# State-space keys: four tiles' sums in one bank, their rows spread by a product, segment sums turned

## The chip, the core and the metric

The kernel is one program on one core of a Trainium2 chip. The metric is the device time of one execution in microseconds (us), the median of several runs. The core has TensorE (PE: matrix products; its weight loads are listed apart as PEld), VectorE (DVE), ScalarE (ACT), GpSimd (POOL), and a queue on SyncE that starts the weight transfers.

## What is computed

Two blocks follow each other, on 256 positions of width 1024: first a block with forgetting attention, selected attention and two layers of retrieved experts, then a block of two layers, each made of a gated feed-forward, a mixer, and another feed-forward. The change touches only the mixer of the second block, which runs twice (stages `ssd0` and `ssd1`):

```python
proj = h @ w_in                                   # z, xbc, dt, q, k, v
dt  = softplus(dt_raw + dt_bias);  adt = dt * -exp(a_log)
a_cum = cumsum(adt)                               # inside chunks of 128 positions, 16 heads
seg   = a_cum[l] - a_cum[s]
lmat  = where(l >= s, exp(seg), 0)
y_diag = einsum(C_l . B_s, lmat, x_s * dt_s)      # 4 groups of 4 heads, 2 chunks
...                                               # state between chunks, gate, norm
q = rms_norm(q per head of 64) ; k = rms_norm(k per head of 64)
y_att = dilated_attention(q, k, v)
x = x + concat(y_ssd, y_att) @ w_out
```

`seg` for a pair l, s is the sum of `adt` over the positions between them, and that is how the kernel makes it: as a product with 0/1 triangles.

## The kernel before

Every weight tile is 128x1024 in float32 (512 KB), streamed by the SyncE queue through a ring of five. ACT copies each tile to a rounded half `HI` (L525), DVE subtracts to get `LOW` (L538), and TensorE multiplies both with the activations `HT`, which are split in the same way: 24 products of 256 columns for a projected tile (`project`, L882), all in the fp32r format. ACT makes HI two tiles ahead and DVE makes LOW one tile ahead of the one being multiplied (`feed`).

There is no scheduler: each engine's order is that of its own program below, and semaphores (`c.by(event)`) tie them. A product's result goes to one of four PSUM banks, P4 to P7, taken first in, first out by `open_bank`; who opens a bank waits until its last reader has freed it. A bank opened with `held=True` is out of the turn until `leave_bank`. P0 to P3 hold long sums.

In a mixer stage the order on TensorE is: norm and turning of the input, 16 tiles `sx`, one `sd` (the steps dt), 8 slots `sz`, and then the loop that the change is in: for i in 0..7 one key tile is projected, one group of four heads gets its segment sums (`segments`, L2736, one bank), and the group before gets its `diagonal` product (L2716). The 8 query tiles follow, then 8 value slots and the attention. Round the loop:

- `steps(i)` on POOL (L3095) makes the moving data of the segment sums: gt times adt for four heads, 128x512. It waits for `segments(i-2)`, since there are two buffers.
- ACT copies the key tile and squares it (L2856, L2857), then takes exp of the segment sums (L2880).
- DVE multiplies that by C.B (`decayed`, L3023), for which `diagonal(i)` waits.
- after every second tile `key_sums(p)` (L2723) sums the squares of two tiles over each head and spreads them over the head's rows in the same product (128x512); DVE makes means of them (L2992), ACT the root (L2862), DVE the reciprocal (L2998) and the scaling of the two key tiles (L3000).
- at the loop's start DVE copies dt and adt out of PSUM (L2977) and makes `xd` = x dt for both chunks (L2985); ACT's first key copy waits for the second of these, and its exp `ea` of the cumulated steps (L2874) comes after that; POOL's `xe` (L3110) waits for `ea`.

Of the kernel before, what the change touches and what calls it, by code (L numbers as in the profile page):

```python
# [28 lines left out]
def shape_constants():  # L29
# [1328 lines left out]
def arena_parts(s, places):  # L1358
# [7 lines left out]
    if s[:3] == "ssd":  # L1366
        return [[("a", 26624 + places[s]["width"], F32), ("h", 4096, F32R), ("l", 4096, F32R)]]
# [1290 lines left out]
def ssd_tensor(pe, c, s):  # L2658
# [65 lines left out]

    for i in range(8):
# [86 lines left out]
def ssd_scalar(act, c, s):  # L2812
# [51 lines left out]
    for i in range(8):
# [64 lines left out]
def ssd_vector(dve, c, s):  # L2929
# [58 lines left out]
    def key_means(p):  # L2988
        dve.wait_ge(*c.by(s, "key_sums", p))
        if p >= 2:  # L2990
            dve.wait_ge(*c.by(s, "keys_normed", p - 2))
        dve.tensor_scalar(f.rr2[p % 2], c.psum(s, "key_sums", p), 1.0 / 64, EPS, ALU.mult, ALU.add).then_inc(  # L2992
            *c.dve.at((s, "key_means", p), ("free", s, "key_sums", p)))

    def key_norm(p):
        rr = f.rr2[p % 2]
        dve.wait_ge(*c.by(s, "key_root", p))
        dve.reciprocal(rr, rr).then_inc(*c.dve.at((s, "key_inverse", p)))  # L2998
        dve.wait_ge(*c.by(s, "key_inverse", p))
        dve.scalar_tensor_tensor(out=f.pair(p), in0=f.pair(p), scalar=f.gain, in1=rr, op0=ALU.mult,  # L3000
                                 op1=ALU.mult).then_inc(*c.dve.at((s, "keys_normed", p)))
# [12 lines left out]
    for i in range(8):  # L3014
# [218 lines left out]
```

## Time and profile before

| | us |
|---|---|
| median of 3 runs | 3196.69 (3194.41 to 3196.91) |
| profiled execution, its own time | 3195.49 |
| its span, first to last instruction | 3193.7 |
| PE busy in the span | 3140.6 (98%) |
| DVE busy | 2531.2 (79%) |
| ACT busy | 1682.2 (53%) |
| POOL busy | 466.6 (15%) |

The span is a profile of one execution. An engine's busy time counts its instructions' durations, waits for a shared resource inside an instruction included. The loop that the change is in takes 2216.7 to 2264.9 us in the first mixer stage and comes again 621.4 us later in the second, with the same durations to a few hundredths of a microsecond.

### The profile page before, as it was taken

How to read it: one execution, taken by the hardware profiler on the slowest of the kernel's cores; microseconds unless marked ns; L12 is line 12 of the kernel's file. 1: busy time of each engine (PE TensorE's matmuls, PEld its weight loads, DVE VectorE, ACT ScalarE, POOL GpSimd, SP SyncE). 2: the span in 40 equal slices, each digit the busy share in tenths (PEclk: the TensorE clock that was granted, in tenths of full speed). 3: DMA queues.
4: the chain of work that ended last, by engine and by line, in shares of the span. 5: the costliest groups of instructions: out<-in, count | busy, mean ns of one | idle time of the engine just before them, and what ended most of it. 6: DMA issues, size and time to landing. Idle time of an engine off the chain costs nothing.

```text
span 3193.7 us, 52741 instructions
## 1 busy us (share of the span) xinstructions
PE 3140.6 (98%) x20327; PEld 2733.2 (86%) x20327; DVE 2531.2 (79%) x4361; ACT 1682.2 (53%) x2698; POOL 466.6 (15%) x317
## 2 busy tenths in 40 slices
PE   7999999999999999999999999999999999999999
PEld 7799988888888679988888888889978888898787
DVE  7879999888878679999877777758777677687775
ACT  4455555544455564555555555456654454566543
POOL 0268100000000458300000000002140000022200
PEclk9999999999999999999999999999999999999999
DMA  9445455577766225445566555554435555544355
GB/s 346 171 139 182 146 166 178 200 268 254 259 203 247 73 95 185 159 152 178 172 218 213 191 191 177 188 178 164 139 121 190 191 181 187 177 145 151 130 188 171
DMA packets 160312, 579.91 MB, mean 182 GB/s; under 512 B 18368, under 2 KB 20160, under 8 KB 160064
## 3 DMA queue, kind: packets, MB, share of 16 engines
q1 hardware_dynamic: 155952, 567.60, 52.6%
q10 hardware_dynamic: 3600, 8.37, 0.7%
q8 instruction: 164, 2.69, 0.3%
q0 software_dynamic: 512, 0.57, 0.1%
q14 instruction: 84, 0.69, 0.1%
HBM read 574.89 MB, written 1.05 MB: 180 GB/s over the span
## 4 chain that ended last, share of the span: by engine, by line
PE 92%; DVE 5%; issue 1%; ACT 1%; DMA 1%; POOL 0%; ACTq 0%; SPq 0%; DVEq 0%
PE P L2189 22%; PE P L893 17%; PE P L956 12%; PE P L2166 12%; PE P L896 9%; PE P L882 8%; PE P L2153 2%; DVE LOW L538 1%; PE P L861 1%; PE P L920 1%; PE P L1138 1%; PE P L1152 1%; PE P L981 1%; PE P L864 1%; PE P L795 1%
## 5 line engine op out<-in xcount | busy, mean ns | idle before, releaser
L538 DVE TENSOR_TENSOR LOW<-RING,HI 128x1024 fp32r<-128x1024 f32 x880 | 1078.0, 1228 | 152.5 <-ACT HI L525 151.3
L525 ACT ACTIVATE HI<-RING 128x1024 fp32r<-128x1024 f32 x984 | 1032.6, 1052 | 288.2 <-DMA RING<-in_pv 83.8
L893 PE MATMUL P<-HT,HI 128*128 128x512 f32 x2368 | 590.9, 391 | 0.0
L893 PEld LDWEIGHTS P<-HT,HI 128*128 128x128 f32 x2368 | 433.4, 188 | 83.6 <-issue 1.0
L896 PEld LDWEIGHTS P<-HT,LOW 128*128 128x128 f32 x2368 | 323.0, 190 | 23.1
L896 PE MATMUL P<-HT,LOW 128*128 128x256 f32 x2368 | 330.2, 282 | 0.0
L2166 PE MATMUL P<-HT,HI 128*128 128x256 f32 x2048 | 282.4, 286 | 0.0
L538 POOL TENSOR_TENSOR LOW<-RING,HI 128x1024 fp32r<-128x1024 f32 x104 | 252.1, 2431 | 89.0 <-ACT HI L525 88.7
L2166 PEld LDWEIGHTS P<-HT,HI 128*128 128x128 f32 x2048 | 258.7, 192 | 0.1
L882 PE MATMUL P<-HT,HI 128*128 128x256 f32 x1728 | 233.5, 288 | 0.0
L882 PEld LDWEIGHTS P<-HT,HI 128*128 128x128 f32 x1728 | 216.3, 192 | 9.0 <-issue 4.2
L904 DVE TENSOR_REDUCE peer_a<-P 128x256 f32<-128x512 f32 x128 | 88.2, 689 | 108.5 <-PE P L896 108.2
L752 POOL TENSOR_SCALAR STAT<-STAT 128x1 f32<-128x1 f32 x10 | 6.1, 613 | 1068.1 <-DVE STAT L759 564.2
L2472 DVE TENSOR_TENSOR peer_a<-peer_a 128x256 f32<-128x256 f32 x256 | 159.1, 622 | 1.0 <-ACT peer_a L2260 1.0
L2263 ACT ACTIVATE peer_a<-P 128x256 f32<-128x256 f32 x128 | 49.2, 384 | 182.5 <-PE P L2166 182.5
L2166 PE MATMUL P<-HT,LOW 128*128 128x256 f32 x1024 | 143.7, 283 | 0.0
L2189 PE MATMUL P<-LOW,peer_wh 128*128 128x512 f32 x512 | 143.1, 401 | 0.0
L2253 ACT ACTIVATE peer_a<-P 128x512 f32<-128x512 f32 x128 | 76.4, 597 | 125.8 <-PE P L2153 125.8
L631 POOL MEMSET ACC<- 128x1024 f32 x10 | 10.1, 1005 | 893.9 <-PE P L2153 548.6
L2189 PE MATMUL P<-HI,peer_wh 128*128 128x512 f32 x512 | 137.1, 389 | 1.6 <-ACT peer_wh L2272 1.6
L2189 PE MATMUL P<-HI,peer_wl 128*128 128x512 f32 x512 | 136.8, 389 | 0.0
L2189 PE MATMUL P<-HI,peer_wh_latex 128*128 128x512 f32 x496 | 135.5, 394 | 0.0
(437 smaller groups left out, 5315.1 us busy)
## 6 DMA issues: line engine op xcount, KB each, us to landing
RING<-in_pu SPq DMA_DIRECT2D x256, 512.0 KB, 3.3
RING<-in_pv SPq DMA_DIRECT2D x256, 512.0 KB, 3.3
RING<-in_fgA SPq DMA_DIRECT2D x44, 512.0 KB, 3.3
RING<-in_fuA SPq DMA_DIRECT2D x44, 512.0 KB, 3.2
RING<-in_fdA SPq DMA_DIRECT2D x44, 512.0 KB, 3.2
RING<-in_fgB SPq DMA_DIRECT2D x44, 512.0 KB, 3.3
RING<-in_fuB SPq DMA_DIRECT2D x44, 512.0 KB, 3.3
RING<-in_fdB SPq DMA_DIRECT2D x44, 512.0 KB, 3.2
```

Of the source, the lines that this page charges most:

```text
L525: act.activation(c.his[i % NHL], c.raw[m % NR], ACT.Copy).then_inc(*c.hi.at(("hi", m)))
L538: eng.tensor_tensor(c.low[m % NR], c.raw[m % NR], c.his[i % NHL].bitcast(F32), ALU.subtract).then_inc(*sig.at(("lo", m)))
L882: m = pe.matmul(ps[:, 0:256], w[:, k * 128:k * 128 + 128], c.ht[h][:, k, :], start=i == 0 and k == 0, stop=i == 2 and k == 7)
L893: pe.matmul(ps, hi[:, k * 128:k * 128 + 128], c.both[:, :, k, :], start=k == 0, stop=False)
L896: m = pe.matmul(ps[:, 0:256], lo[:, k * 128:k * 128 + 128], c.ht[0][:, k, :], start=False, stop=k == 7)
L904: dve.tensor_reduce(dst, ps, AX.X, ALU.add).then_inc(*c.dve.at(event, ("free", name, j)))
L956: m = pe.matmul(c.y[q], lhs[1 if i == 1 else 0][:, t * 128:t * 128 + 128], (lo if i == 2 else hi)[:, hf * 512:hf * 512 + 512], start=i == ...
L2153: m = pe.matmul(ps[:, 64 * t:64 * t + 64], f.is_row[g % 2][:, t // SIDE, :, t % SIDE], f.share[g % 2][q][:, t // SIDE, :, t % SIDE], start ...
L2166: m = pe.matmul(ps[:, 0:256], w[:, k * 128:k * 128 + 128], c.ht[h][:, k, :], start=i == 0 and k == 0, stop=i == 2 and k == 7)
L2189: m = pe.matmul(c.y[q], (f.wl(j) if i == 1 else f.wh(j))[:, t * 128:t * 128 + 128], (lo if i == 2 else hi)[:, hf * 512:hf * 512 + 512], st ...
L2253: act.activation(dst, c.psum(s, "gates", part, g).rearrange("p (t j) -> p t j", t=8), ACT.Copy, scale=1.0 / SHARE).then_inc(*c.act.at((s, ...
L2472: dve.tensor_tensor(ge, ge, f.gate_of(j), ALU.mult).then_inc(*c.dve.at((s, "weighed", j)))
```

## The change

Four edits, in the mixer stages alone.

1. **Segment sums turned.** The stationary and the moving side change places: gt, as `later`, is the stationary operand once for all heads, and le times adt moves, 128x512 for four heads. The data are now fp32r, and so that nothing is lost adt is split in two parts, `ad2`, both of which go through the product: two products of 512 columns instead of four float32 ones of 128. `steps` on POOL writes 128x1024 instead of 128x512, and DVE makes `ad2` with two small instructions before `xd`. POOL makes `later` (128x128) at the stage's start.
2. **Sums of four tiles in one bank.** `key_sums(i)` runs for each tile with 256 columns; four of them add into one held bank, each tile's heads in rows of its own. The existing helpers `heads_root_scalar` (ACT, L1029 before) and `heads_inverse_vector` (DVE, L1035 before) then take one root and one reciprocal of 256 columns for four tiles.
3. **Rows spread.** `key_rows(p)` spreads the reciprocals back over 128 rows for two tiles: two products of 256 columns in fp32r, on `both_rows`, which holds a rounded part and its remainder in rows of the same tile, made by two DVE instructions after the reciprocal. POOL makes the stationary `rows_of` (128x512) at the stage's start. `key_norm` reads the factors from PSUM.
4. **Room.** The packed constants of a mixer stage (loaded on ACT's queue in the feed-forward before) grow by 737 columns of float32.

```diff
@@ Ssd
-        self.wb = [c.at(s, 24576 + 512 * n, 512) for n in range(2)]
+        steps = c.arena[s, "h"]
+        self.wb = [steps[:, 1024 * n:1024 * n + 1024] for n in range(2)]
+        self.later = c.arena[s, "l"][:, 0:128]
+        self.ad2 = c.arena[s, "l"][:, 128:192]
@@ ssd_tensor
-    def key_sums(p):
-        ps = open_bank(pe, c, s, "key_sums", p)
-        pe.wait_ge(*c.by("squares", f.sqk, 8 + 2 * p + 1))
-        pe.matmul(ps, bd64, f.sq2[p % 2], start=True, stop=True).then_inc(*c.pe.at((s, "key_sums", p)))
+    def key_sums(i):
+        j = 8 + i
+        b, q = divmod(j, 4)
+        if q == 0:
+            open_bank(pe, c, "heads_sums", f.sqk, b, held=True)
+        pe.wait_ge(*c.by("squares", f.sqk, j))
+        pe.matmul(c.psum("heads_sums", f.sqk, b)[:, 0:256], f.pack("headsum")[:, 96 - 32 * q:224 - 32 * q], f.sq[j % 4],
+                  start=q == 0, stop=q == 3).then_inc(*c.pe.at(("head_sums", f.sqk, j)))
+        if q == 3:
+            leave_bank(c, "heads_sums", f.sqk, b)
+
+    def key_rows(p):
+        b, half = divmod(p, 2)
+        ps = open_bank(pe, c, s, "key_rows", p)
+        pe.wait_ge(*c.by(s, "both_rows", b))
+        pe.wait_ge(*c.by(s, "rows_of"))
+        for q in (2 * half, 2 * half + 1):
+            m = pe.matmul(ps[:, q % 2 * 256:q % 2 * 256 + 256], f.rows_of[:, 128 * q:128 * q + 128], f.both_rows[b],
+                          start=True, stop=True)
+        m.then_inc(*c.pe.at((s, "key_rows", p)))
...
-        for r in range(4):
-            m = pe.matmul(ps[:, r * 128:r * 128 + 128], f.wb[i % 2][:, r * 128:r * 128 + 128], f.le, start=True, stop=True)
+        for half in range(2):
+            m = pe.matmul(ps, f.later, f.wb[i % 2][:, 512 * half:512 * half + 512], start=half == 0, stop=half == 1)
...
-        if i >= 2 and i % 2 == 0:
-            key_sums(i // 2 - 1)
+        if i:
+            key_sums(i - 1)
+        if i == 7:
+            key_rows(0)
     project(pe, c, f.sqk, 0)
     diagonal(7)
...
-    key_sums(3)
+    key_sums(7)
+    key_rows(1)
...
+        if j in (3, 4):
+            key_rows(j - 1)
@@ ssd_scalar
-        if i >= 2 and i % 2 == 0:
-            key_root(i // 2 - 1)
+        if i == 5:
+            heads_root_scalar(act, c, f.sqk, 2, f.rr[0], c.const("eps"))
...
         if j == 0:
-            key_root(3)
+            heads_root_scalar(act, c, f.sqk, 3, f.rr[1], c.const("eps"))
@@ ssd_vector
+    dve.wait_ge(*c.by(s, "dt"))
+    dve.tensor_copy(f.ad2[:, 0:32], f.dts[:, 32:64]).then_inc(*c.dve.at())
+    dve.wait_ge(*c.dve.last())
+    dve.tensor_tensor(f.ad2[:, 32:64], f.dts[:, 32:64], f.ad2[:, 0:32].bitcast(F32), ALU.subtract).then_inc(
+        *c.dve.at((s, "steps_halves")))
...
+    def key_inverse(b):
+        rr = f.rr[b]
+        heads_inverse_vector(dve, c, f.sqk, 2 + b, rr)
+        dve.wait_ge(*c.by("heads_inverse", f.sqk, 2 + b))
+        dve.tensor_copy(f.rr_hi, rr).then_inc(*c.dve.at())
+        dve.wait_ge(*c.dve.last())
+        dve.scalar_tensor_tensor(out=f.both_rows[b], in0=f.rr_hi.bitcast(F32), scalar=f.pack("lowrow"), in1=rr,
+                                 op0=ALU.mult, op1=ALU.add).then_inc(*c.dve.at((s, "both_rows", b)))
...
-        if i >= 3 and i % 2:
-            key_norm(i // 2 - 1)
...
-        if i >= 2 and i % 2 == 0:
-            key_means(i // 2 - 1)
+        if i == 6:
+            key_inverse(0)
...
         if j == 0:
-            key_means(3)
+            key_norm(0)
+            key_norm(1)
             carried(0)
             carried(1)
+        if j == 1:
+            key_inverse(1)
...
-        if j == 4:
-            key_norm(3)
+        if j in (4, 5):
+            key_norm(j - 2)
@@ ssd_pool
-        pool.tensor_tensor(f.wb[i % 2].rearrange("p (r s) -> p r s", r=4), f.gt.unsqueeze(1).broadcast_to([128, 4, 128]),
-                           f.ad[:, ch, 4 * g:4 * g + 4].unsqueeze(2).broadcast_to([128, 4, 128]), ALU.mult).then_inc(
+        ad = f.ad2.bitcast(F32).rearrange("p (q t h) -> p q t h", q=2, t=2)[:, :, ch, 4 * g:4 * g + 4]
+        pool.tensor_tensor(f.wb[i % 2].rearrange("p (q r l) -> p q r l", q=2, r=4),
+                           f.le.unsqueeze(1).unsqueeze(1).broadcast_to([128, 2, 4, 128]),
+                           ad.unsqueeze(3).broadcast_to([128, 2, 4, 128]), ALU.mult).then_inc(
             *c.pool.at((s, "steps", i)))
 
     pool.wait_ge(*c.by(s, "legt"))
+    pool.tensor_tensor(f.later, f.gt, f.gt, ALU.mult).then_inc(*c.pool.at((s, "later")))
+    pool.wait_ge(*c.by(s, "pack"))
+    pool.tensor_scalar(f.rows_of, f.pack("hsel2"), 1.0, None, ALU.mult).then_inc(*c.pool.at((s, "rows_of")))
...
-    pool.wait_ge(*c.by(s, "dt"))
+    pool.wait_ge(*c.by(s, "steps_halves"))
     steps(0)
     steps(1)
```

Three places in the order of the instructions. First POOL, from the norm of a mixer stage (L752 before, L756 after) to the loop, as it stands before:

```order
L752 TENSOR_SCALAR STAT<-STAT 128x1 [waits s_pool_done,s_act_done,s_dve_done,s_pe_done]
L3102 TENSOR_TENSOR ssd_a<-ssd_a 128x1024 [waits s_pool_done,s_tables_landed,s_act_done,s_dve_done,s_pe_done]
L3102 TENSOR_TENSOR ssd_a<-ssd_a 128x1024 [waits s_act_done]
L3095 TENSOR_TENSOR ssd_a<-ssd_a 128x512 [waits s_dve_done]
L3095 TENSOR_TENSOR ssd_a<-ssd_a 128x512
L3110 TENSOR_TENSOR ssd_a<-ssd_a 128x1024 [waits s_act_done,s_dve_done]
```

and with the change (L3135 is `later`, L3137 `rows_of`, L3129 `steps`, L3148 `xe`):

```order
L756 TENSOR_SCALAR STAT<-STAT 128x1 [waits s_pool_done,s_act_done,s_dve_done,s_pe_done]
L3135 TENSOR_TENSOR ssd_l<-ssd_a 128x128 [waits s_pool_done,s_act_done,s_tables_landed,s_dve_done,s_pe_done]
L3137 TENSOR_SCALAR ssd_l<-ssd_a 128x512 [waits s_pack_landed]
L3140 TENSOR_TENSOR ssd_a<-ssd_a 128x1024 [waits s_act_done] x2
L3129 TENSOR_TENSOR ssd_h<-ssd_a,ssd_l 128x1024 [waits s_dve_done]
L3129 TENSOR_TENSOR ssd_h<-ssd_a,ssd_l 128x1024
L3148 TENSOR_TENSOR ssd_a<-ssd_a 128x1024 [waits s_act_done,s_dve_done]
```

Two instructions now stand right behind the norm's, and each `steps` is twice as wide.

Second DVE at the start of the loop, before (L2977 takes dt out of PSUM, L2985 makes `xd`, L538 makes LOW of the second key tile, L3023 is `decayed(0)`):

```order
L2977 COPY ssd_a<-P 128x64 [waits s_pe_done]
L2985 TENSOR_TENSOR ssd_a<-ssd_a 128x1024 [waits s_act_done,s_dve_done]
L2985 TENSOR_TENSOR ssd_a<-ssd_a 128x1024 [waits s_act_done]
L538 TENSOR_TENSOR LOW<-RING,HI 128x1024 [waits s_hi_made]
L3023 TENSOR_TENSOR ssd_a<-ssd_a 128x512 [waits s_dve_done,s_act_done]
```

and with the change:

```order
L3004 COPY ssd_a<-P 128x64 [waits s_pe_done]
L3006 CAST ssd_l<-ssd_a 128x32 [waits s_dve_done]
L3008 TENSOR_TENSOR ssd_l<-ssd_a,ssd_l 128x32 [waits s_dve_done]
L3017 TENSOR_TENSOR ssd_a<-ssd_a 128x1024 [waits s_act_done,s_dve_done]
L3017 TENSOR_TENSOR ssd_a<-ssd_a 128x1024 [waits s_act_done]
L542 TENSOR_TENSOR LOW<-RING,HI 128x1024 [waits s_hi_made]
L3053 TENSOR_TENSOR ssd_a<-ssd_a 128x512 [waits s_dve_done,s_act_done]
```

Two small instructions came in ahead of `xd`.

Third TensorE from the segment sums of i = 5 to the key tile of i = 6, before (L2736 segment sums, L2716 diagonal product, L882 a projected tile; P4 to P7 are the banks):

```order
L2736 MATMUL P7<-ssd0_a 128x128 [waits s_pool_done,s_act_done]
L2736 MATMUL P7<-ssd0_a 128x128 x3
L2716 MATMUL P2<-ssd0_a 128x64 [waits s_act_done,s_dve_done]
L2716 MATMUL P2<-ssd0_a 128x64 x3
L882 MATMUL P6<-HT,HI 128x256 [waits s_hi_made,s_act_done]
```

and with the change, from the last sum of the first four tiles on (L2735 is `key_sums`, L2761 the segment sums, L2725 the diagonal product, L886 a projected tile):

```order
L2735 MATMUL P6<-ssd0_a 128x256 [waits s_act_done]
L886 MATMUL P7<-HT,HI 128x256 [waits s_hi_made,s_act_done]
L886 MATMUL P7<-HT,HI 128x256 x15
L886 MATMUL P7<-HT,LOW 128x256 [waits s_lo_made]
L886 MATMUL P7<-HT,LOW 128x256 x7
L2761 MATMUL P4<-ssd0_h,ssd0_l 128x512 [waits s_pool_done,s_act_done]
L2761 MATMUL P4<-ssd0_h,ssd0_l 128x512
L2725 MATMUL P2<-ssd0_a 128x64 [waits s_act_done,s_dve_done]
L2725 MATMUL P2<-ssd0_a 128x64 x3
L2735 MATMUL P5<-ssd0_a 128x256 [waits s_act_done]
L886 MATMUL P6<-HT,HI 128x256 [waits s_hi_made,s_act_done]
```

The key tile of i = 6 now goes into P6, the bank in which the sums of the first four tiles stood, and whose reader is ACT's root at i = 5.

## Rows read from the trace of the kernel before

**Rows 1.** The page: busy us, share of the span, instructions.

```profile
PE 3140.6 (98%) x20327; PEld 2733.2 (86%) x20327; DVE 2531.2 (79%) x4361; ACT 1682.2 (53%) x2698; POOL 466.6 (15%) x317
```

**Rows 2.** The chain of waits from 2215 to 2275 us: start us, us, what.

```profile
2214.83 1.59 PE P L956 x7
...
2229.20 0.89 PE P L2736 x8
...
2230.94 1.78 PE P L2747 x8
...
2233.58 2.87 PE P L882 x24
...
2242.84 0.91 PE P L2723 x2
...
2247.51 0.84 PE P L2716 x8
...
2264.93 2.87 PE P L882 x24
```

**Rows 3.** Timeline at the loop's start, DVE, POOL, ACT: start us, us, engine, line.

```profile
2216.80 0.23 DVE L2977 COPY ssd_a<-P 128x64 f32<-128x64 f32 x1 [2.39 <-PE P L2703]
2217.06 3.21 DVE L2985 TENSOR_TENSOR ssd_a<-ssd_a 128x1024 f32<-128x1024 f32 x2
2217.11 4.06 POOL L3095 TENSOR_TENSOR ssd_a<-ssd_a 128x512 f32<-128x512 f32 x2 [10.00 <-DVE ssd_a L2977]
...
2220.19 2.06 DVE L538 TENSOR_TENSOR LOW<-RING,HI 128x1024 fp32r<-128x1024 f32 x1
2220.35 0.38 ACT L2856 ACTIVATE ssd_a<-P 128x256 f32<-128x256 f32 x1 [2.09 <-DVE ssd_a L2985]
...
2222.32 0.20 ACT L2874 ACTIVATE ssd_a<-P 128x32 f32<-128x32 f32 x1
...
2222.66 1.91 POOL L3110 TENSOR_TENSOR ssd_a<-ssd_a 128x1024 f32<-128x1024 f32 x1 [1.49 <-ACT ssd_a L2874]
...
2223.04 2.07 DVE L3023 TENSOR_TENSOR ssd_a<-ssd_a 128x512 f32<-128x512 f32 x1 [0.79 <-ACT ssd_a L2880]
```

**Rows 4.** The instructions of L3095 and L2985: ns min/median/max.

```profile
L3095 POOL TENSOR_TENSOR ssd_a<-ssd_a x16: 1041/1265/2082, 2217.1 to 2869.0; 128x512 f32<-128x512 f32 x16
...
L2985 DVE TENSOR_TENSOR ssd_a<-ssd_a x4: 1224/1643/2064, 2217.1 to 2839.6; 128x1024 f32<-128x1024 f32 x4
```

**Rows 5.** Timeline of ACT in the loop at i = 5.

```profile
2251.66 0.38 ACT L2857 ACTIVATE ssd_a<-P 128x256 f32<-128x256 f32 x1
2252.21 0.60 ACT L2880 ACTIVATE ssd_a<-P 128x512 f32<-128x512 f32 x1 [0.17 <-PE P L2736]
2252.82 1.28 ACT L2862 ACT_TABLE_LOAD   x1
```

**Rows 6.** ACT's root of 256 columns in the first block.

```profile
L1029 ACT ACTIVATE mix_a<-P,mix_a x5: 455/475/478, 104.0 to 1055.3; 128x256 f32<-128x256 f32 x5
```

**Rows 7.** Timeline at the mixer stage's norm.

```profile
2136.50 0.76 POOL L752 TENSOR_SCALAR STAT<-STAT 128x1 f32<-128x1 f32 x1 [189.00 <-DVE STAT L759]
...
2137.89 0.56 DVE L767 TENSOR_SCALAR ssd_a<-X,STAT 128x640 f32<-128x640 f32 x1
...
2138.57 1.04 PE L795 MATMUL P<-CST,ssd_a 128*128 128x128 f32 x8
```

**Rows 8.** Timeline at the first stage's norm.

```profile
10.37 1.47 POOL L631 MEMSET ACC<- 128x1024 f32 x1
...
11.08 1.10 DVE L767 TENSOR_SCALAR mix_a<-X,STAT 128x640 f32<-128x640 f32 x1
```

**Rows 9.** POOL's instructions of L1345, L1346, L538: ns min/median/max.

```profile
L1345 POOL TENSOR_SCALAR mix_a<-mix_a,STAT x40: 604/606/1500, 133.4 to 1141.3; 128x128 f32<-128x128 f32 x40
...
L1346 POOL TENSOR_SCALAR mix_a<-mix_a,STAT x40: 922/927/1677, 134.1 to 1141.9; 128x256 f32<-128x256 f32 x40
...
L538 POOL TENSOR_TENSOR LOW<-RING,HI x104: 2377/2406/2916, 164.3 to 1312.2; 128x1024 fp32r<-128x1024 f32 x104
```

More of the change, by code:

```diff
@@ L38, in shape_constants @@
     c["bd64"] = (p[:, None] // 64 == p[None, :] // 64).astype(f)
+    c["headsum"] = np.zeros((128, 224), f)
+    c["headsum"][:, 96:128] = c["bd64"][:, 48:80]
+    c["hsel2"] = 2 * c["hsel"]
+    c["lowrow"] = -(p[:, None] % 16 // 8).astype(f)
     c["le"] = (p[:, None] <= p[None, :]).astype(f)
@@ L1366, in arena_parts @@
     if s[:3] == "ssd":
-        return [[("a", 26624 + places[s]["width"], F32), ("h", 4096, F32R), ("l", 4096, F32R)]]
+        return [[("a", 25600 + places[s]["width"], F32), ("h", 4096, F32R), ("l", 4096, F32R)]]
     return [[("a", 32768, F32), ("ij", 512, F16), ("g2", 512, F16), ("iota", 128 * SIDE, F16), ("iota16", 128, F16),
@@ L2627, in __init__ @@
         self.sq = [c.at(s, 4096 + 256 * n, 256) for n in range(4)]
-        self.sq2 = [c.at(s, 4096 + 512 * n, 512) for n in range(2)]
         self.junk = c.at(s, 5120, 1024)
-        self.rr2 = [c.at(s, 22024 + 512 * n, 512) for n in range(2)]
+        self.rr = [c.at(s, 22024 + 256 * n, 256) for n in range(2)]
         self.d = [c.at(s, 23048 + 256 * n, 256) for n in range(5)]
@@ L2637, in __init__ @@
         self.ad = self.dts[:, 32:64].rearrange("p (t h) -> p t h", t=2)
-        self.wb = [c.at(s, 24576 + 512 * n, 512) for n in range(2)]
-        self.eb = [c.at(s, 25600 + 512 * n, 512) for n in range(2)]
-        self.pack = lambda n: c.packed(s, s, 26624, n if n == "bd64" else f"{n}_{l}")
+        steps = c.arena[s, "h"]
+        self.wb = [steps[:, 1024 * n:1024 * n + 1024] for n in range(2)]
+        self.later = c.arena[s, "l"][:, 0:128]
+        self.ad2 = c.arena[s, "l"][:, 128:192]
+        self.eb = [c.at(s, 24576 + 512 * n, 512) for n in range(2)]
+        self.pack = lambda n: c.packed(s, s, 25600, n if n in ("bd64", "headsum", "hsel2", "lowrow") else f"{n}_{l}")
+        self.both_rows = [c.arena[s, "l"][:, 192 + 256 * n:448 + 256 * n] for n in range(2)]
+        self.rr_hi = c.arena[s, "l"][:, 704:960]
+        self.rows_of = c.arena[s, "l"][:, 1024:1536]
         self.an, self.gain = c.stat(4, 1), c.stat(5, 1)
@@ L2806, in ssd_loads @@
 def ssd_loads(act, c, s):
-    act.dma_start(c.at(s, 26624, c.places[s]["width"]), c.ins[f"pack_{s}"]).then_inc(*c.landed["pack"].at((s, "pack")))
+    act.dma_start(c.at(s, 25600, c.places[s]["width"]), c.ins[f"pack_{s}"]).then_inc(*c.landed["pack"].at((s, "pack")))
     act.dma_start(c.at(s, 18944, 256), c.ins["legt"]).then_inc(*c.landed["tables"].at((s, "legt")))
@@ L2869, in ssd_scalar @@
         if i >= 4:
-            act.wait_ge(*c.by(s, "key_sums", i // 2 - 2))
+            act.wait_ge(*c.by("head_sums", f.sqk, 4 + i))
         copied(8 + i, f.kt[:, i, :])
@@ L2986, in ssd_vector @@
                           ALU.mult).then_inc(*c.dve.at((s, "xd", t)))
[L2988 to L2993, printed above, removed]
-    def key_norm(p):
[L2996 to L3001, printed above, removed]
+    def key_inverse(b):
[6 more added lines that the diff above has]
+                                 op0=ALU.mult, op1=ALU.add).then_inc(*c.dve.at((s, "both_rows", b)))
+    def key_norm(p):
+        dve.wait_ge(*c.by("copied", f.sqk, 8 + 2 * p + 1))
+        dve.wait_ge(*c.by(s, "key_rows", p))
+        dve.scalar_tensor_tensor(out=f.pair(p), in0=f.pair(p), scalar=f.gain, in1=c.psum(s, "key_rows", p), op0=ALU.mult,
+                                 op1=ALU.mult).then_inc(*c.dve.at((s, "keys_normed", p), ("free", s, "key_rows", p)))
     def gate(t, hf):
```

7 lines of the change are left out of this document (2 added, 5 removed).

## The prediction

> **What bounds the kernel now.** I read the page first: TensorE is busy for 98% of the span and POOL for 15% [rows 1], so time is TensorE's products plus its few waits. Then the chain of waits over the loop of the first mixer stage: it runs from one TensorE group to the next with almost nothing between. A projected tile costs 2.87 us for 24 products (0.12 each of 256 columns), a group's segment sums 0.89, the diagonal product 0.84, a key sum of 512 float32 columns 0.91, four float32 products of 256 columns 1.78 (0.445 each), and seven fp32r products of 512 columns 1.59 (0.23 each) [rows 2]. Last the timeline, for what stands around TensorE [rows 3, 5, 7]. The work of DVE and ACT that goes (reciprocals and roots of 512 columns) is hidden behind TensorE and is worth nothing by itself. Both mixer stages behave alike, so I cost one and take it twice.
>
> **TensorE's own work.** Segment sums: four float32 products of 128 columns at 0.89 become two fp32r products of 512 columns, 2 x 0.23 = 0.46. That is 0.43 less, eight times: **-3.4 us**. Key sums: four of 0.91 are 3.6, eight of 0.445 are 3.6: **0**. Key rows are new: eight fp32r products of 256 columns at 0.12: **+1.0**. If nothing waited, a stage would gain 2.4 us, and two stages 4.9.
>
> **A mechanism that the rest hangs on.** DVE and POOL do not run side by side here. POOL's two `steps` of 128x512 took 4.06 us together at the loop's start, while DVE's two `xd` took 3.21 [rows 3]; the same instructions take 1.04 and 1.22 each elsewhere [rows 4]. The four ran by turns: xd(0) to 2218.3, steps(0) to 2219.2, xd(1) to 2220.3, steps(1) to 2221.2. L538 behind them took 2.06, where `xd` of the same width takes 1.22, and `decayed(0)` took 2.07, since it was held until POOL's `xe` ended at 2224.57 [rows 3]. Whoever waits longer goes first, and then needs its own time less about 0.14 that was spent at the door.
>
> **Wait 1, the loop's start.** `steps` is now 128x1024, which the trace does not show. The nearest is `xe`, also 128x1024 with a repeated operand: 1.91 [rows 3]. So 0.87 more for each, which DVE sees in full. Ahead of `xd` DVE gets two small instructions, about 0.4 us with hand-off, by the 0.23 of the copy before them [rows 3]. I follow the turns:
> - xd(0) ends at 2218.6, steps(0) at 2220.4 (TensorE was ready for it at 2220.0), xd(1) at 2221.5, steps(1) at 2223.2, and LOW of the second key tile at 2224.3 instead of 2222.25.
> - TensorE: segment sums 2220.45 to 2220.9, the HI part of the next tile until 2222.85, then it stands for LOW until 2224.35, 1.5 us; tile done at 2225.35, next sums at 2225.8.
> - `ea` comes 1.2 later, since ACT's first copy waits for xd(1); `xe` gets its turn after LOW and ends at 2226.1, `decayed(0)` at 2226.65. In the trace it ended at 2225.11 [rows 3]: the diagonal product starts **1.5 us later**, even though two groups of segment sums (2 x 0.43) are already saved.
> - On to the fourth key tile: third sums save 0.43, two small key sums stand for one large, and `decayed(1)`, behind two more wide `steps`, costs about 0.35. That tile started at 2233.58 [rows 2]; I get 2234.95, 1.35 later. With the three savings of 0.43 that makes waits of **+2.7 us**.
> From there POOL has 4.6 us a turn for 1.9 of work, and `steps` is ahead again.
>
> **Wait 2, a bank.** The sums of the first four tiles stay in P6 until ACT's root at i = 5 has read them, and the key tile of i = 6 opens just P6. In the trace ACT squares the tile (0.38), takes exp (0.60), and loads the table for the root at once behind it, 1.28 us [rows 5]. Ahead of the square lies a copy of the same tile, about 0.3. Counted from the end of the key tile of i = 5: square done at 0.7, exp at 1.3, table 2.55, root 3.0 (0.475 for 256 columns [rows 6]). TensorE is through its sums (0.46), diagonal (0.84 [rows 2]) and key sum (0.445) at 1.75. It stands **+1.3 us**. Before, the root read no bank, and this wait did not exist.
>
> **Wait 3, the norm.** At the stage's start POOL now runs `later` and `rows_of` right behind its norm instruction, which ends at 2137.26; DVE's L767 is issued at 2137.89 and TensorE's second turning waits for it [rows 7]. `later` ends near 2137.7, so `rows_of` is under way when L767 comes. That this pair collides the first stage shows: with a POOL instruction from 10.37 to 11.84, L767 took 1.10 instead of 0.56 [rows 7, 8]. `rows_of` is a TENSOR_SCALAR of 512 columns: 128 columns take 0.604 and 256 take 0.922 [rows 9], so 512 take 1.56. Floor: POOL's 1.47 [rows 8] is a memset of 1024 columns, so 512 could take half, 0.73. L767 then ends 1.25 or 0.4 later. If DVE slips in between the two, it is nothing. I take the nearest kind, **+1.25 us**.
>
> **Hidden.** DVE's new instructions at i = 6 (reciprocal of half the columns, cast, combination, some 2.3 us) end about 0.6 us before `key_rows(0)` needs them. At j = 0 `carried` reopens the bank of `key_rows(0)` just as `key_norm(0)` frees it, with 0.2 us to spare. The larger constants load, 377 KB more, lies in the feed-forward before and goes beside a ring of five tiles. If any of these covers were gone, it would cost tenths.
>
> **The sum.** One stage: -3.4 + 0 + 1.0 + 2.7 + 1.3 + 1.25 = +2.8; with the unrounded values 2.7. Two stages: +5.4. The profiled execution took 3195.49, which makes 3200.9; the median of the runs is 1.2 above it, so there 3202.1.
>
> **Rivals.**
> - *Forecast, all three waits*, 3202 with a range of 3199 to 3206: 0.50. About 6 of 10 of it lies below the mark of +0.2%.
> - *The norm wait is small or absent*, because `rows_of` runs at half the memset's time or DVE goes first. Then 2 x 0.85 to 2 x 1.25 less, about 3200, and down to 3197 if the small casts are cheap as well: 0.25. For it: only 0.2 us decide who goes first.
> - *Waits hidden, the arithmetic counts*: two stages at -2.4 and some tenths that TensorE now stands at `decayed(0)`, 3191. It needs LOW of the second key tile and the root in time, and both rows speak against that: 0.05.
> - *Slower*: a wide `steps` takes more than 1.9. POOL's L538, with two full operands, takes 2.38 [rows 9]. Four `steps` lie on the path at the loop's start, so 0.1 more for each is 0.4 in a stage and 0.8 in all. From 2.04 us for each the kernel is over the mark, and at 2.4 it takes 3206: 0.20. Against it: `steps` repeats both operands, and at 512 columns took 1.04, which with `xe` at 1.91 lies on one line.
>
> The Trainium skill's page "GPSIMD Engine Reference", section "Elementwise — side-by-side cycle accounting", would have the slower case: it measures a float32 `tensor_tensor` of 2048 columns on this engine at 4.5 us, as an estimate 2.25 for 1024. By that the sum would be +2.8 us more, 3205. The trace's `xe` took 1.91 for that width [rows 3], so I keep the row.
>
> **How the numbers follow.** What a measurement of this kernel can tell from no change is about 0.2%, 6.4 us: 3190.3 and 3203.1. Of the forecast 0.31 lies within and 0.19 over; the small norm wait adds 0.25 within; the slower rival 0.20 less a little over; the hidden case 0.04 faster, and the rest within. Faster 0.04, same 0.60, slower 0.36. The range leaves out the hidden case below and the worst of the slow one: 3194 to 3208.
>
> **What the profile will show.** Segment sums at 0.46 and eight key sums at 0.445; POOL's 128x1024 `steps` at 1.9 alone and 3 and more beside DVE; PE idle before the LOW part of the second key tile, about 1.5, released by DVE; PE idle of 1.3 before the key tile of i = 6, released by ACT's root; L767 at 1.0 to 1.8 in mixer stages. Wrong it would be if the first wait is not there, since it is half of the waits; if ACT loads the root's table elsewhere; or if TensorE's granted clock falls in the gaps.

## The result: 4.6 us longer, a ratio of 1.0016

The changed kernel took 3200.75 us (median of 18 runs, 3197.81 to 3204.94), the kernel before 3196.12 (18 runs beside it, 3191.55 to 3197.89). The ratio is 1.0016, with a 95% interval of 1.0009 to 1.0022: slower by 4.6 us, and inside the 0.2% that the forecast called the same. The forecast was 3202.1. The profiled execution took 3199.65, with a span of 3197.8.

The page of after; the first row answers to [rows 1]. Busy time of DVE and ACT fell by 9 and 16 us, that of POOL rose by 18. None of the three says what happened to the time.

```profile
PE 3137.5 (98%) x20263; PEld 2729.2 (85%) x20263; DVE 2522.1 (79%) x4361; ACT 1666.6 (52%) x2686; POOL 484.3 (15%) x321
```

The chain of waits of after over the same loop as in [rows 2] (start us, us, what). The fourth key tile starts at 2234.23; counted from the first key tile it started 16.88 in before and starts 18.41 in after (the first tiles start at 2216.70 and 2215.82 in the two timelines). A group of segment sums is 0.47 instead of 0.89, a key sum 0.49 twice for 0.91 once, and key rows are 0.23. From the fourth key tile on one stretch leaves TensorE: from 2246.45 to 2249.44 the chain lies on ACT. (Over the first three tiles it lies mostly on DVE.)

```profile
2233.79 0.43 PE P L2735 x2
2234.23 2.87 PE P L886 x24
2237.09 0.47 PE P L2761 x2
2237.56 0.84 PE P L2725 x8
2238.40 0.49 PE P L2735 x2
...
2247.04 0.61 ACT ssd_a L2907
2247.66 1.28 ACT L1033
2248.96 0.48 ACT ssd_a L1033
2249.44 0.04 issue
2249.48 3.13 PE P L886 x24
...
2259.06 0.23 PE P L2746 x2
```

The waits of TensorE in the same loop of after (us in total, times, longest). In before this view had one row, 0.2 us of L2716 for L3023.

```profile
PE P L886 <- ACT ssd_a L1033: 1.3, 1, 1.3
PE P L886 <- DVE LOW L542: 1.2, 1, 1.2
PE P L2725 <- DVE ssd_a L3053: 0.8, 2, 0.6
PE P L2761 <- POOL ssd_h L3129: 0.3, 1, 0.3
```

The timeline of after at the loop's start, TensorE, DVE and POOL; it answers to [rows 3]. TensorE's HI part of the second key tile ends at 2222.24 and its LOW part starts at 2223.45, since L542 runs from 2220.49 to 2223.41: it shares the time with the second wide `steps` (L3129) and then with `xe` (L3148). The first `decayed` (L3053) takes 2.37 beside `xe`.

```profile
2216.51 4.05 DVE L3017 TENSOR_TENSOR ssd_a<-ssd_a 128x1024 f32<-128x1024 f32 x2
2220.49 2.92 DVE L542 TENSOR_TENSOR LOW<-RING,HI 128x1024 fp32r<-128x1024 f32 x1
2223.34 2.37 DVE L3053 TENSOR_TENSOR ssd_a<-ssd_a 128x512 f32<-128x512 f32 x1
...
2216.67 5.65 POOL L3129 TENSOR_TENSOR ssd_h<-ssd_a,ssd_l 128x1024 fp32r<-128x1024 f32 x2 [10.42 <-DVE ssd_l L3008]
2222.96 2.21 POOL L3148 TENSOR_TENSOR ssd_a<-ssd_a 128x1024 f32<-128x1024 f32 x1 [0.64 <-ACT ssd_a L2901]
...
2220.16 2.08 PE L886 MATMUL P<-HT,HI 128*128 128x256 f32 x16
2223.45 1.21 PE L886 MATMUL P<-HT,LOW 128*128 128x256 f32 x8 [1.22 <-DVE LOW L542]
2224.51 0.63 PE L2761 MATMUL P<-ssd_h,ssd_l 128*128 128x512 f32 x2
2225.76 1.11 PE L2725 MATMUL P<-ssd_a 128*128 128x64 f32 x8 [0.63 <-DVE ssd_a L3053]
```

At the norm the timeline of after (DVE, then POOL) answers to [rows 7]: L771 is issued at 2136.80, 0.17 after `rows_of` (L3137) began, and takes 0.79, not 0.56. It ends at 2137.59, half a microsecond before `rows_of` does.

```profile
2136.80 0.79 DVE L771 TENSOR_SCALAR ssd_a<-X,STAT 128x640 f32<-128x640 f32 x1
...
2135.42 0.76 POOL L756 TENSOR_SCALAR STAT<-STAT 128x1 f32<-128x1 f32 x1 [189.00 <-DVE STAT L763]
2136.26 0.40 POOL L3135 TENSOR_TENSOR ssd_l<-ssd_a 128x128 fp32r<-128x128 f32 x1
2136.63 1.51 POOL L3137 TENSOR_SCALAR ssd_l<-ssd_a 128x512 fp32r<-128x512 f32 x1
```

**A table by stage.** The runs of one kernel spread over 7 us, so single effects of a microsecond are read from the traces. I took the first start of five kinds of TensorE work in the first mixer stage of each profiled execution, and of the norm after it; the second stage agrees within 0.1 us. Columns are us: the norm's turning to the first cumulative sum, to the first state product, to the first `carried`, to the turning of y, to the next stage's norm, and the sum. The medians stand last.

| kernel | to sums | to states | to carried | to y | to norm | stage | median |
|---|---|---|---|---|---|---|---|
| before | 82.4 | 11.1 | 32.2 | 31.0 | 88.0 | 244.7 | 3196.12 |
| after | 82.5 | 13.0 | 31.8 | 31.4 | 88.5 | 247.2 | 3200.75 |
| root ahead of exp | 82.5 | 13.1 | 30.1 | 31.5 | 88.4 | 245.6 | 3197.02 |
| steps at half width | 82.5 | 11.4 | 31.8 | 31.4 | 88.5 | 245.6 | 3197.54 |
| copies behind skip | 82.3 | 13.1 | 31.7 | 31.4 | 88.5 | 247.0 | 3201.11 |
| segment sums alone | 82.3 | 13.0 | 30.7 | 30.9 | 88.0 | 244.9 | 3196.84 |
| keys alone | 82.3 | 11.5 | 33.8 | 31.4 | 88.4 | 247.4 | 3201.14 |
| 31 columns | 82.6 | 13.0 | 31.8 | 31.4 | 88.0 | 246.8 | 3199.04 |
| three edits | 82.4 | 13.0 | 30.2 | 31.4 | 88.0 | 245.0 | 3195.78 |
| and `xd` late | 82.4 | 10.2 | 30.1 | 31.3 | 88.0 | 242.0 | 3191.07 |

The stage of after is 2.5 us longer than that of before, 5.0 for two; the medians say 4.6. TensorE's granted clock was 1.00 in the loop of both (2216 to 2264), so it did not fall in the gaps.

### The profile page after: what moved, and what is told of

It reads as the page before. It is cut to its first block, busy times and chain, and to the rows that moved or that the text cites. A ratio compares the mean times of both kernels' runs of the same rounds, so it can differ in the third digit from the quotient of the medians.

```text
span 3197.8 us, 52611 instructions
## 1 busy us (share of the span) xinstructions
PE 3137.5 (98%) x20263; PEld 2729.2 (85%) x20263; DVE 2522.1 (79%) x4361; ACT 1666.6 (52%) x2686; POOL 484.3 (15%) x321
## 3 DMA queue, kind: packets, MB, share of 16 engines
HBM read 575.64 MB, written 1.05 MB: 180 GB/s over the span
## 4 chain that ended last, share of the span: by engine, by line
PE 91%; DVE 5%; issue 1%; ACT 1%; DMA 1%; POOL 0%; SPq 0%; DVEq 0%; ACTq 0%
PE P L2193 22%; PE P L897 17%; PE P L960 12%; PE P L2170 11%; PE P L900 9%; PE P L886 8%; PE P L2157 2%; DVE LOW L542 1%; PE P L865 1%; PE P L924 1%; PE P L1142 1%; PE P L1156 1%; PE P L985 1%; PE P L868 1%; PE P L799 1%
## 5 line engine op out<-in xcount | busy, mean ns | idle before, releaser
L542 DVE TENSOR_TENSOR LOW<-RING,HI 128x1024 fp32r<-128x1024 f32 x880 | 1081.2, 1231 | 150.9 <-ACT HI L529 150.4
L542 POOL TENSOR_TENSOR LOW<-RING,HI 128x1024 fp32r<-128x1024 f32 x104 | 252.0, 2429 | 89.1 <-ACT HI L529 88.9
L886 PE MATMUL P<-HT,HI 128*128 128x256 f32 x1728 | 231.7, 287 | 2.6 <-ACT ssd_a L1033 2.6
L886 PEld LDWEIGHTS P<-HT,HI 128*128 128x128 f32 x1728 | 216.5, 192 | 9.8 <-ACT ssd_a L1033 3.4
L756 POOL TENSOR_SCALAR STAT<-STAT 128x1 f32<-128x1 f32 x10 | 6.1, 612 | 1068.4 <-DVE STAT L763 564.3
L2264 ACT ACTIVATE peer_a<-peer_a 128x256 f32<-128x256 f32 x128 | 53.2, 416 | 165.8 <-DVE peer_a L908 165.8
```

The lines of the kernel that those rows point to most:

```text
L542: eng.tensor_tensor(c.low[m % NR], c.raw[m % NR], c.his[i % NHL].bitcast(F32), ALU.subtract).then_inc(*sig.at(("lo", m)))
L886: m = pe.matmul(ps[:, 0:256], w[:, k * 128:k * 128 + 128], c.ht[h][:, k, :], start=i == 0 and k == 0, stop=i == 2 and k == 7)
```

## The experiments

Each was run beside the kernel before; the first four together (before: 3195.94 there, 33 runs), the last four together (3195.75, 33 runs), each kernel 11 times. A diff shows the edit's core.

**Root ahead of exp.** Is TensorE's wait at i = 6 the bank that the root holds?

```diff
@@ ssd_scalar, for i in range(8)
         feed(act, c, "act", f.sqk, 8 + i)
+        if i == 5:
+            heads_root_scalar(act, c, f.sqk, 2, f.rr[0], c.const("eps"))
...
-        if i == 5:
-            heads_root_scalar(act, c, f.sqk, 2, f.rr[0], c.const("eps"))
```

> ACT takes the root of the first four tiles at the start of i = 5, ahead of that tile's copy, instead of behind its exp. Theory (the bank P6 is held by a late root): the wait of 1.3 us before the key tile of i = 6 is gone in both stages, with nothing in its place, since the table loads now fall into the time of the projection: 2.6 us less than the changed kernel, about 3198.2. Rival (the lost time lies in the arithmetic of key sums and key rows, or in transfers, and TensorE would only wait elsewhere): no change, 3200.8.

3197.02, ratio 1.0008 (0.9998 to 1.0017); the stretch to `carried` is 1.7 us shorter. The chain of this run goes through the place on TensorE alone:

```profile
2245.45 0.84 PE P L2725 x8
2246.28 0.49 PE P L2735 x2
2246.77 2.86 PE P L886 x24
2249.64 0.47 PE P L2761 x2
```

The bank was the wait. It gave back 1.6 per stage, more than the 1.3 that the view of waits lists, and than the 1.3 that I had expected.

**Steps at half width.** What do the wide `steps` cost at the loop's start? POOL makes only the first half of each, and both products read that half, so the second part of the step sizes is not in the sums.

```diff
-        pool.tensor_tensor(f.wb[i % 2].rearrange("p (q r l) -> p q r l", q=2, r=4),
-                           f.le.unsqueeze(1).unsqueeze(1).broadcast_to([128, 2, 4, 128]),
-                           ad.unsqueeze(3).broadcast_to([128, 2, 4, 128]), ALU.mult)
+        pool.tensor_tensor(f.wb[i % 2][:, 0:512].rearrange("p (r l) -> p r l", r=4),
+                           f.le.unsqueeze(1).broadcast_to([128, 4, 128]),
+                           ad[:, 0, :].unsqueeze(2).broadcast_to([128, 4, 128]), ALU.mult)
...
-            m = pe.matmul(ps, f.later, f.wb[i % 2][:, 512 * half:512 * half + 512], start=half == 0, stop=half == 1)
+            m = pe.matmul(ps, f.later, f.wb[i % 2][:, 0:512], start=half == 0, stop=half == 1)
```

> POOL writes only the first half of the steps (128x512); both products read that half, so TensorE's work is the same and the segment sums are twice the rounded part. Theory (DVE and POOL take turns, and the wide steps push xd, LOW and decayed back): steps take 1.04 alone, the wait for LOW of the second key tile falls from 1.2 to under 0.5, the fourth key tile starts 1.6 us sooner in each stage: 3.2 us less, about 3197.6. Rival (the two small DVE instructions and the order of the queues make the wait, whatever POOL's width): under 0.5 us less, 3200.5.

3197.54, ratio 1.0004 (0.9995 to 1.0013); the stretch to the states is 1.6 shorter. The wait for LOW is gone; that for the first `decayed` is longer than in after:

```profile
PE P L886 <- ACT ssd_a L1033: 1.3, 1, 1.3
PE P L2725 <- DVE ssd_a L3053: 1.2, 1, 1.2
```

So the width is 1.6 of what the loop's start costs. The rest stays with `steps` of the old width. In this run's timeline the first `decayed` is issued 0.80 after DVE fell idle, waiting for ACT's exp, and takes 2.07 beside `xe`, as in before (0.79 and 2.07 in [rows 3]); counted from the first key tile it comes 6.67 in, where it came 6.34 in before. TensorE gets there two groups of segment sums sooner, 0.84, and waits.

**Copies behind skip.** The two small products of POOL at the stage's start go behind its products with the skip weights.

```diff
@@ ssd_pool
     pool.wait_ge(*c.by(s, "legt"))
-    pool.tensor_tensor(f.later, f.gt, f.gt, ALU.mult).then_inc(*c.pool.at((s, "later")))
-    pool.wait_ge(*c.by(s, "pack"))
-    pool.tensor_scalar(f.rows_of, f.pack("hsel2"), 1.0, None, ALU.mult).then_inc(*c.pool.at((s, "rows_of")))
     for t in range(2):
...
+    pool.tensor_tensor(f.later, f.gt, f.gt, ALU.mult).then_inc(*c.pool.at((s, "later")))
+    pool.wait_ge(*c.by(s, "pack"))
+    pool.tensor_scalar(f.rows_of, f.pack("hsel2"), 1.0, None, ALU.mult).then_inc(*c.pool.at((s, "rows_of")))
     pool.wait_ge(*c.by(s, "steps_halves"))
```

> POOL makes later and rows_of after the two skip products, when it is idle before the loop, instead of behind the norm. By the trace of the changed kernel L771 took 0.79 in mixer stages and 0.55 elsewhere, so 0.2 us less in each stage, 0.4 in all, about 3200.3, and L771 back at 0.55. By the price in my prediction, where the loser stands for the whole of rows_of, it would be 2.5 us less, 3198.3.

3201.11, ratio 1.0013 (1.0004 to 1.0022); the stage is 0.2 shorter. L771 of this run, beside that of after (ns min/median/max), is back at its time without company:

```profile
L771 DVE TENSOR_SCALAR ssd_a<-X,STAT x2: 553/554/556, 2139.1 to 2762.9; 128x640 f32<-128x640 f32 x2
```

```profile
L771 DVE TENSOR_SCALAR ssd_a<-X,STAT x2: 783/786/790, 2136.8 to 2760.8; 128x640 f32<-128x640 f32 x2
```

The collision costs 0.2 and not 1.25: at that price this kernel would have stood near 3198.3. And it is not `rows_of` as such that holds L771 back. The run with the keys alone (below) has no `later`; there `rows_of` (L3129 in that kernel) starts 0.54 ahead of L771 and runs a microsecond past its issue, and L771 takes 0.55, its time alone:

```profile
2137.08 1.56 POOL L3129 TENSOR_SCALAR ssd_l<-ssd_a 128x512 fp32r<-128x512 f32 x1
2137.62 0.55 DVE L771 TENSOR_SCALAR ssd_a<-X,STAT 128x640 f32<-128x640 f32 x1
```

In the run with the segment sums alone `later` stands by itself, ends 0.15 before the same DVE instruction (L767 there), and that takes 0.56. Only with `later` and `rows_of` one behind the other, where L771 comes 0.17 into `rows_of`, is it longer. Why it is then was not tested.

**Segment sums alone.** The kernel before with part 1 of the change (turned products, `ad2`, wide `steps`, `later`) and its own keys.

```diff
@@ before, Ssd; its sq2, rr2, key_sums, key_means, key_root and key_norm stay
-        self.wb = [c.at(s, 24576 + 512 * n, 512) for n in range(2)]
+        steps = c.arena[s, "h"]
+        self.wb = [steps[:, 1024 * n:1024 * n + 1024] for n in range(2)]
+        self.later = c.arena[s, "l"][:, 0:128]
+        self.ad2 = c.arena[s, "l"][:, 128:192]
```

> The kernel before with the turned segment sums alone (later, ad2, wide steps), the key part as it was. Theory: arithmetic -3.4 us in a stage, waits at the loop's start +2.9, no bank wait: about -0.6 in a stage, 1.2 us under the kernel before, near 3195. If the waits at the start were no property of the wide steps, it would gain the whole 3.4 in a stage, 3189.5.

3196.84, ratio 0.9999 (0.999 to 1.0008): the stage is 0.2 longer than before, not 0.6 shorter. The miss is on DVE. The chain of this run, from the fifth `decayed` on:

```profile
2245.72 1.72 DVE ssd_a L3031
2247.44 0.60 DVE ssd_a L3000
2248.04 1.13 DVE LOW L538
2249.17 3.27 DVE ssd_a L3006
2252.45 0.03 issue
2252.47 0.06 DVE ssd_a L3008
2252.53 0.61 issue
2253.14 0.69 DVE ssd_a L3031
```

L3006 is the reciprocal of 512 columns. I had called this work hidden and worth nothing; that holds only while TensorE's pass is as long as it was. With the passes shorter DVE becomes the last to arrive: TensorE waits three times for `decayed` (0.63, 0.62, 0.25; 1.5 in all), where after waits twice (0.63, 0.21). The third wait ends at 2263.33, and the chain above stays on DVE until then, over a second such reciprocal (2258.62): the key part takes the 3.35 us reciprocals away, and that wait with them, which its own arithmetic does not show. The second ends at 2233.60, before the first reciprocal (2239.12). It is longer than in after because after has a small key sum to do there: counted from the first key tile both kernels pass this wait at 15.09.

**Keys alone.** The counterpart: after with the segment sums, the `steps` and the room of before.

```diff
@@ after, Ssd and arena_parts; no ad2, no later
-        self.wb = [steps[:, 1024 * n:1024 * n + 1024] for n in range(2)]
+        self.wb = [c.at(s, 25600 + c.places[s]["width"] + 512 * n, 512) for n in range(2)]
...
-        return [[("a", 25600 + places[s]["width"], F32), ("h", 4096, F32R), ("l", 4096, F32R)]]
+        return [[("a", 26624 + places[s]["width"], F32), ("h", 4096, F32R), ("l", 4096, F32R)]]
```

> The kernel of after with the segment sums of before (steps of 512 columns, four products, no halves of the steps, no copy of gt); the key part of the change stays whole. It is the counterpart of the run with the segment sums alone. If the two parts only add up, this kernel takes after's 3200.75 less what the segment part alone cost (0.2 per stage there) and stands at 3200.4. By the terms as the trace of after has them: key rows +1.0, key sums +0.36, bank held for the root +1.0 to 1.3, norm +0.15, attention +0.5, together +3.1 per stage, 3202.3. Rival, by the shadow on VectorE that the segment part alone ran into: the two parts help each other (the short products need VectorE relieved of the reciprocals), and the keys alone lose the 3.4 of shorter products as well as keep their own cost, but not wait 1: again +3.1. The steps of 1.9 us being gone, the key tiles at the loop's start stand as in before. Forecast 3201.5, between 3200.3 and 3202.5; under 3199 the key part is not what costs.

3201.14, ratio 1.0021 (1.0012 to 1.003); the stage is 2.7 longer than before. With 0.2 for the segment sums alone the parts add up to 2.9 against the 2.5 of both together. The key part is what costs: TensorE waits 1.1 for the root here too, has the key rows to do, and its arenas start as in after. The small key sums cost nothing: with segment sums of the old kind two passes take 10.17 (2233.30 to 2243.47 in the chain of this run), as in before (2233.58 to 2243.75).

**31 columns.** After, with 31 unused columns at the end of the first arena, so that `ssd_h` and `ssd_l` behind it start at the same byte modulo 128 as in before. No instruction differs.

```diff
-        return [[("a", 25600 + places[s]["width"], F32), ("h", 4096, F32R), ("l", 4096, F32R)]]
+        return [[("a", 25600 + places[s]["width"] + 31, F32), ("h", 4096, F32R), ("l", 4096, F32R)]]
```

> The kernel of after with 31 unused columns at the end of the arena ssd_a, so that the arenas ssd_h and ssd_l start at the same place modulo 128 bytes as in before; no instruction is changed. Theory: in after and in the three runs made from it the products whose stationary is ssd_h or ssd_l take 396 to 398 ns against 392 to 394 in before and in the run with the segment sums alone, about 0.5 us per mixer stage, since the change moved these arenas to a start that is no multiple of 16 bytes. It expects 1.0 less in all, 3199.7, and medians of 392 to 394 ns for those products. Rival: the start does not matter (the slower products come from what runs beside them, as the banks of the state-space keys), and the time stays at 3200.7 with 396 to 398 ns.

3199.04, ratio 1.0015 (1.0006 to 1.0024). The ratio alone does not tell it from after. The stretch to the next norm does: 87.96 and 87.97 in the two stages, as in before (87.98, 87.97), against 88.45 in both. The other kernels bear it out. By their code the first arena is a multiple of 16 bytes long in segment sums alone, three edits and the last run, and the stretch is 87.95 to 87.98 there; it is not in root ahead of exp, steps at half width, copies behind skip and keys alone, and there it is 88.45 to 88.48. The products with `ssd_h` and `ssd_l` show it one by one (ns min/median/max from 2300 to 2400 us). First after, then this run:

```profile
L960 PE MATMUL P<-HI,ssd_h x56: 392/397/497, 2314.2 to 2371.2; 128*128 128x512 f32 x56
L960 PE MATMUL P<-HI,ssd_l x56: 393/394/399, 2315.3 to 2372.2; 128*128 128x512 f32 x56
L960 PE MATMUL P<-LOW,ssd_h x56: 390/394/399, 2316.2 to 2373.1; 128*128 128x512 f32 x56
```

```profile
L960 PE MATMUL P<-HI,ssd_h x56: 388/395/504, 2311.5 to 2368.1; 128*128 128x512 f32 x56
L960 PE MATMUL P<-HI,ssd_l x56: 387/392/395, 2312.6 to 2369.0; 128*128 128x512 f32 x56
L960 PE MATMUL P<-LOW,ssd_h x56: 387/392/397, 2313.5 to 2369.9; 128*128 128x512 f32 x56
```

Two nanoseconds in each of 168 products are 0.34 of the 0.49 us. The 24 like products of L924 behind them (medians 396, 396 and 397 ns in after, 392, 394 and 388 here, eight of each) are another 0.12. The segment sums, which read both operands from the same arenas, stayed at a median of 396 ns; they gained nothing.

**Three edits.** The root ahead of exp, the copies behind skip and the 31 columns together in after. The question is whether the gains add up.

> The kernel of after with the first root of the keys put ahead of the exponential of its pass, the copy of gt and of the spread matrix put behind the skip products on GpSimd, and the 31 unused columns. If the gains add up (1.6 + 0.2 + 0.5 per stage), it takes 4.6 less than after and stands at 3196.1, level with before. Rival: the root's place and the others share one wait (what the root gives back is waited for elsewhere), and it stays over 3197.

3195.78, ratio 1.0002 (0.9993 to 1.0011). The stage is 2.2 shorter than after's, where 1.6 + 0.2 + 0.4 adds up to 2.2. Against before the stage is 0.3 longer: the loop's start still takes 13.0 for 11.1 and the stretch to y 31.4 for 31.0, while the one to `carried` is 2.0 shorter.

**And `xd` late.** In the kernel with three edits DVE's second product with dt goes behind the third `decayed`; the squares of the tiles get 1024 columns of their own, so that ACT need not wait for it.

```diff
-        self.sq = [c.at(s, 4096 + 256 * n, 256) for n in range(4)]
+        self.sq = [c.at(s, 25600 + c.places[s]["width"] + 256 * n, 256) for n in range(4)]
@@ ssd_scalar
-        if i == 0:
-            act.wait_ge(*c.by(s, "skip", 1))
-            act.wait_ge(*c.by(s, "xd", 1))
@@ ssd_vector, in the loop behind decayed(i); xd(0) stays ahead of the loop
+        if i == 2:
+            scaled(1)
```

> The kernel of the run with the three edits, and in it the second product of VectorE with dt (xd of the second half, 2.0 us beside GpSimd) moved behind the third decayed tile, with the squares of the key tiles put in columns of their own, so that ScalarE need not wait for it. Theory of wait 1: TensorE waits at the loop's start (1.2 for the LOW of the second key tile, 0.6 for the first decayed tile) since VectorE has two products with dt ahead of them while the wide steps take turns with it. With one of them gone LOW is there about 2 us earlier and the first exponential 1.5 us earlier: 1.5 to 1.8 less per stage, 3.0 to 3.6 in all, 3192.8 if the run with three edits stands at 3196.1, and so below before. Rival: the product of 2 us is only waited for later, since VectorE is full over the first three passes (LOW 1.2 to 2.9, decayed 1.1 to 2.4 each); then the time does not move by more than 0.5.

3191.07, ratio 0.9989 (0.998 to 0.9998): 4.7 us faster than before, and as much faster than the run with three edits. The stretch to the states is 10.2, 2.8 shorter, and the stage 3.0; I had expected 1.5 to 1.8. By the medians the edit is worth 4.7 us, by the two stages 6.0. The product and ACT's wait for it were moved together, so what each is worth is not shown. TensorE's part of the timeline, as above for after: the one wait left in the loop is 0.3 for the first `steps`.

```profile
2221.59 0.70 PE L2761 MATMUL P<-ssd_h,ssd_l 128*128 128x512 f32 x2 [0.32 <-POOL ssd_h L3130]
2222.13 2.07 PE L886 MATMUL P<-HT,HI 128*128 128x256 f32 x16
2224.03 1.12 PE L886 MATMUL P<-HT,LOW 128*128 128x256 f32 x8
2224.99 0.63 PE L2761 MATMUL P<-ssd_h,ssd_l 128*128 128x512 f32 x2
2225.46 1.00 PE L2725 MATMUL P<-ssd_a 128*128 128x64 f32 x8
```

The same edit in the kernel before was not run. TensorE waits 0.2 there in the whole loop, so I would expect little from it.

## Why the prediction came out right, and where it did not

The forecast said +5.4 for two stages and the traces show +5.0. The sum is nearer than its terms: a miss of 1.05 in each stage was for the greater part made good by a wait that was too low (0.3) and a cost that was not seen (0.4 to 0.5). That part of the agreement is luck. Per stage, by its own steps:

| step | predicted | measured | from |
|---|---|---|---|
| segment sums | -3.4 | -3.4 | 0.89 to 0.47, eight times |
| key sums | 0 | 0 | two passes 10.17 in before and in keys alone |
| key rows | +1.0 | +0.9 | four of 0.23 or 0.24 |
| wait 1, loop start | +2.7 | +2.7 | 13.0 - 11.1, without 3 x -0.42 and one key sum |
| wait 2, bank | +1.3 | +1.6 | root ahead of exp |
| wait 3, norm | +1.25 | +0.2 | copies behind skip |
| operand's place | not seen | +0.4 to 0.5 | 31 columns |
| sum | +2.7 | +2.4 to 2.5 | stage table: +2.5 |

- *Key sums*: a single one shows at 0.49 in the chain and not at 0.445, but the projected tile behind it shows at 2.87 and not 2.93. Two of them cost what the one of 0.91 did.
- *Wait 1* was right in place, releasers and size: 1.22 idle before LOW (1.5 forecast), the first diagonal product 1.47 later (1.5 forecast), and the fourth key tile 1.53 later, where 1.35 was forecast. The wide `steps` took 1.90 alone (the shortest of L3129: 1895 ns), as `xe` had shown, and so the rival with dearer `steps` is out. The price of the page "GPSIMD Engine Reference" of the Trainium skill (section "Elementwise — side-by-side cycle accounting", 2.25 by the prediction's estimate) is not what this trace shows.
- *Wait 2* came at the place and with the table load (1.28) and root (0.48) that were costed; the run without it gave back 0.3 more than its idle time.
- *Wait 3* is the step that failed. Its wording was "`later` ends near 2137.7, so `rows_of` is under way when L767 comes", and that is what happened. But L767 was then taken to stand until `rows_of` ends. It took 0.23 longer, and ended before `rows_of` did; in keys alone it took no longer at all beside the same `rows_of`. The first stage's 1.10 against 0.56 [rows 8] stood beside a memset, and was carried over to another kind of instruction. The rival "the norm wait is small or absent" is what came true in this term, while the total stayed in the first case through the others.
- *Hidden*: DVE's reciprocal, cast and combination at i = 6 ran from 2255.92 to 2258.51, and `key_rows(0)` started 0.55 later behind a key sum, without a wait.
- The prediction said of DVE's saved work that it "is worth nothing by itself". Once the passes are shorter that no longer holds: segment sums alone has a wait of 0.25 for `decayed` behind a reciprocal that after does not have. It is one reason why the two parts cost 2.9 apart and 2.5 together; another is that the first small key sum falls into a wait.

What stays open: which alignment the arenas need, since modulo 128 bytes only two starts occur, 4 apart, and why the segment sums did not profit; when a POOL instruction holds L771 back and when not; and which half of the last edit gave its 3.0.

## What to carry to other kernels

When a change shortens what the bounding engine does in a pass, price the pass anew for the engines beside it: the 3.4 us a stage that the turned segment sums saved went into waits to the last tenth, behind engines that had been hidden. A PSUM bank of a ring is held until its last reader is through; where that reader stands behind other work of its engine, as the root did behind a copy, a square and an exp, move it to the head of the pass (1.6 a stage here). The first passes of a loop need another order than the rest: one product of 2 us that TensorE did not need for three passes, moved out of the way with ACT's wait for it, was worth 4.7 us, as much as the whole change had cost.

## What the runs showed of the hardware

- **A stall of TensorE costs more than the idle time that the profile lists.** At the loop's start of after the idle times are 1.22, 0.63 and 0.21, 2.06 together; the stretch without them is 2.8 shorter (13.0 to 10.2). In the two timelines the LOW part starts 3.29 after the HI part in after and 1.90 without the wait, which is 1.39 for 1.22 listed; the group of products behind the stall takes another 0.1 (1.21 for 1.12). The bank wait likewise: 1.3 listed, 1.6 given back. Groups of products overlap by some 0.17 in the timeline, and a wait breaks the overlap.
- **DVE and POOL share in more than one way.** The DVE product of two tensors L542 took 2.92 behind a `steps` that was under way (2220.49) and 1.21 with POOL idle (2234.21 in the timeline of after). Where both started at once DVE kept its 1.21 and POOL's product took 2.97 for 1.90, which is standing by turns:

```profile
2230.78 2.97 POOL L3129 TENSOR_TENSOR ssd_h<-ssd_a,ssd_l 128x1024 fp32r<-128x1024 f32 x1 [0.47 <-PE P L2761]
2230.78 1.21 DVE L542 TENSOR_TENSOR LOW<-RING,HI 128x1024 fp32r<-128x1024 f32 x1
```

The product with one tensor and a scalar, L771, took 0.79 for 0.55 beside a POOL instruction of 1.51 that began 0.17 ahead of it and ended 0.55 after it, and 0.55 beside one of the same kind that began 0.54 ahead of it (keys alone). The Trainium skill's page "SBUF — State Buffer", section "SBUF: two separate sides", says that the pair of ports is locked for the whole instruction, with the loser fully blocked; it names two-input operations and the fast modes on DVE's side. L542 and L3053 agree with that here, L771 does not.
- **Where an operand starts matters to TensorE.** Products whose stationary operand (in `ssd_h` or `ssd_l`; the moving one, a weight tile, stays where it was) starts at another offset were 2 ns longer of 392. The same page's section "Specifications (TRN2)" says that memory is read in lines of 16 bytes, each new line at a price. It fits, since the arenas' lengths in after are no multiple of 16 bytes and in before are; the runs show only that moving the start by 124 bytes brings the time back, and that the segment sums do not follow.
